# First mixer: squares' sums folded by VectorE and moved into the second row; row factors spread by one-pass products of two parts

## The reference, cut to what matters

```
def rms_norm(x, g):
    xf = x.astype(jnp.float32)
    y = xf * lax.rsqrt(jnp.mean(xf * xf, axis=-1, keepdims=True) + RMS_EPS)
    return (y * g.astype(jnp.float32)).astype(x.dtype)

hn = rms_norm(h, norm_mix[i])
qkv = (xn @ w_qkv).reshape(B, S, 3, N_HEADS, HEAD_DIM)      # A
q = apply_rope(qkv[:, :, 0], cos, sin)
...
h = rmsnorm(x, mix_norm[i])                                  # POOL
x = x + pool_mixer(h, pool_w[j], pool_b[j], pool_scale[j])
```

## Time and profile before

| | |
|---|---|
| median of 3 runs | 1062.39 us (1062.37 to 1062.58) |
| the profiled execution | 1062.58 us |
| its span, first to last instruction | 1060.8 us |
| PE busy | 1056.1 us |
| DVE busy | 835.5 us |
| ACT busy | 649.2 us |
| mean granted clock of TensorE | 1.000 |

### The profile page before, as it was taken

One profiled execution on the slowest core, in us unless ns is written; L12 is line 12 of the kernel. 1 busy time (PEld: TensorE's weight loads), 2 busy tenths in 40 slices (PEclk: granted clock), 3 DMA queues, 4 the chain that ended last, 5 costly groups with the idle time before them and its releaser, 6 DMA issues.

```text
span 1060.8 us, 16688 instructions
## 1 busy us (share of the span) xinstructions
PE 1056.1 (100%) x6764; PEld 941.3 (89%) x6764; DVE 835.5 (79%) x1329; ACT 649.2 (61%) x904; POOL 1.3 (0%) x8
## 2 busy tenths in 40 slices
PE   9999999999999999999999999999999999999998
PEld 8999888888898898888889888888988898888888
DVE  6896899786667789987667999876658768999851
ACT  7665587564367757765557577654557755766540
POOL 0000000000000000000000000000000000000000
PEclk9999999999999999999999999999999999999999
DMA  8554356555525165655652466565555533655540
GB/s 312 196 199 160 119 199 238 199 176 194 170 101 189 54 240 189 223 199 188 218 189 80 156 217 229 183 218 189 181 187 182 175 129 127 233 203 207 203 159 25
DMA packets 32237, 191.83 MB, mean 181 GB/s; under 512 B 4512, under 2 KB 6304, under 8 KB 12320
## 3 DMA queue, kind: packets, MB, share of 16 engines
q1 hardware_dynamic: 32016, 190.49, 51.2%
q10 hardware_dynamic: 144, 0.26, 0.1%
HBM read 189.69 MB, written 1.05 MB: 180 GB/s over the span
## 4 chain that ended last, share of the span: by engine, by line
PE 99%; DMA 0%; DVE 0%; ACT 0%; SPq 0%; issue 0%; DVEq 0%
PE banks L474 22%; PE TB L474 12%; PE SB L474 12%; PE banks L476 12%; PE TB L476 6%; PE SB L476 6%; PE banks L433 4%; PE banks L434 3%; PE banks L435 3%; PE banks L703 3%; PE banks L704 3%; PE banks L716 3%; PE banks L644 2%; PE banks L697 1%; PE banks L699 1%; PE banks L711 1%
## 5 line engine op out<-in xcount | busy, mean ns | idle before, releaser
L1737 DVE TENSOR_TENSOR wlo<-raw,whi 128x2048 fp32r<-128x2048 f32 (+2 forms) x180 | 395.8, 2202 | 77.3 <-ACT whi L1206 77.3
L1206 ACT ACTIVATE whi<-raw 128x2048 fp32r<-128x2048 f32 (+2 forms) x180 | 330.3, 1840 | 84.2 <-PE TB L476 24.7
L474 PE MATMUL banks<-xx,whi 128*128 128x512 f32 x752 | 262.1, 390 | 0.0
L476 PE MATMUL banks<-xx,wlo 128*128 128x256 f32 x752 | 212.2, 282 | 0.0
L474 PEld LDWEIGHTS banks<-xx,whi 128*128 128x128 f32 x752 | 141.2, 188 | 29.3
L476 PEld LDWEIGHTS banks<-xx,wlo 128*128 128x128 f32 x752 | 142.3, 189 | 0.0
L474 PE MATMUL TB<-xx,whi 128*128 128x512 f32 x336 | 117.8, 390 | 0.2 <-DVE xx L1742 0.2
L474 PE MATMUL SB<-xx,whi 128*128 128x512 f32 x320 | 111.8, 390 | 0.0
L476 PE MATMUL TB<-xx,wlo 128*128 128x256 f32 x336 | 94.8, 282 | 0.0
L474 PE MATMUL banks<-hx,whi 128*128 128x512 f32 x264 | 91.7, 390 | 0.0
L476 PE MATMUL SB<-xx,wlo 128*128 128x256 f32 x320 | 90.3, 282 | 0.0
(11 more groups left out here) (272 smaller groups left out, 2027.5 us busy)
## 6 DMA issues: line engine op xcount, KB each, us to landing
raw<-in_gate SPq DMA_DIRECT2D x44, 1024.0 KB, 4.8
raw<-in_up SPq DMA_DIRECT2D x44, 1024.0 KB, 4.8
raw<-in_down SPq DMA_DIRECT2D x32, 1024.0 KB, 4.8
raw<-in_down SPq DMA_DIRECT2D x16, 768.0 KB, 4.4
raw<-in_d_kq SPq DMA_DIRECT2D x8, 1024.0 KB, 4.9
raw<-in_a_kq SPq DMA_DIRECT2D x6, 1024.0 KB, 5.7
raw<-in_a_o SPq DMA_DIRECT2D x4, 1024.0 KB, 5.6
raw<-in_b_o SPq DMA_DIRECT2D x4, 1024.0 KB, 4.8
```

Of the source, the lines that this page charges most:

```text
L474: e.matmul(po[:, 0:512], wh[:, k, sl], a[:, kk, :, :].rearrange("p w s -> p (w s)"), start=start, stop=stop, skip_group_check=True)
L476: return e.matmul(po[:, 0:256], wl[:, k, sl], a[:, kk, 0, :], start=False, stop=stop, skip_group_check=True)
L1206: e.activation(whi[n % RING][:, 0:nk * w], raw[n % RAW][:, 0:nk * w], ACT.Copy).then_inc(s_hi, 1)
L1737: e.tensor_tensor(wlo[n % RING][:, 0:nk * w], raw[n % RAW][:, 0:nk * w], whi[n % RING][:, 0:nk * w].bitcast(F32), ALU.subtract).then_inc(s ...
```

## The change

In A, VectorE adds the two lines of `ssum` (a fold) before it splits the last quarter of weight unit 2; `norm_sums(A)` becomes the two products that B and DD use, and goes from before chunk 2 of slot 1 to the middle of chunk 1, between the products of the two token halves. In A and POOL the factor is rounded (copy into `rr`, part 0), the rest taken (part 1), both on VectorE (`norm_parts`), and `dg` becomes [128, 2, 256] fp32r: the identity scaled by each part, 256 columns each. `row` becomes two fp32r products of 256 columns that add up in `TB`. `dg` grows by 1024 bytes in a partition and `rr` takes 32 bytes behind it.

```diff
-        dg = sb("dg", [128, 2, 128])
+        dg = sb("dg", [128, 2, 256], F32R)
+        rr = sb("rr", [128, 2, 4], F32R)
...
-        FOLD = {B: 1, DD: 4}
+        FOLD = {A: 1, B: 2, DD: 5}
...
             def norm_sums(s):
                 e.wait_ge(s_ones, 1)
-                if s != A:
-                    e.wait_ge(s_fold, FOLD[s])
-                    for h in range(2):
-                        last = e.matmul(SB[:, 0, h:h + 1], ssum[:, 0, h * 128:(h + 1) * 128], ones[:, 0:1],
-                                        start=(h == 0), stop=True, skip_group_check=True)
-                    last.then_inc(s_sum, 1)
-                else:
-                    e.wait_ge(s_add, n_add(s, 3))
-                    token_sums(ssum, SB[:, 0, :]).then_inc(s_sum, 1)
+                e.wait_ge(s_fold, FOLD[s])
+                for h in range(2):
+                    last = e.matmul(SB[:, 0, h:h + 1], ssum[:, 0, h * 128:(h + 1) * 128], ones[:, 0:1],
+                                    start=(h == 0), stop=True, skip_group_check=True)
+                last.then_inc(s_sum, 1)
...
             def row(s, q):
+                e.wait_ge(s_ones_r, 1)
                 e.wait_ge(s_dg, 1 if s == A else 2)
-                e.matmul(TB[:, q, 0:128], ones[:, :], dg[:, 0, :], start=True, stop=True, skip_group_check=True)
-                e.matmul(TB[:, q, 128:256], ones[:, :], dg[:, 1, :], start=True, stop=True,
+                e.matmul(TB[:, q, 0:256], ones_r[:, :], dg[:, 0, :], start=True, stop=False, skip_group_check=True)
+                e.matmul(TB[:, q, 0:256], ones_r[:, :], dg[:, 1, :], start=False, stop=True,
                          skip_group_check=True).then_inc(s_row, 1)
...
-                        if i == 1 and k == (2 if s == A else 0):
+                        if i == 1 and k == 0 and s != A:
                             norm_sums(s)
...
                         high(i, 0, k)
+                        if i == 1 and k == 1 and s == A:
+                            norm_sums(s)
                         high(i, 1, k)
...
-            e.wait_ge(s_rc, 1)
-            for h in range(2):
-                last = e.activation(dg[:, h, :], ident, ACT.Copy, scale=rcol[:, h:h + 1])
+            e.wait_ge(s_rr, 1)
+            for part in range(2):
+                for h in range(2):
+                    last = e.activation(dg[:, part, h * 128:(h + 1) * 128], ident, ACT.Copy,
+                                        scale=rr[:, part, h:h + 1].bitcast(F32))
...
+            def norm_parts(s, col):
+
+                e.wait_ge(s_rc, COL[s])
+                kept(e.tensor_copy(rr[:, 0, 0:2], col))
+                after_own()
+                e.tensor_tensor(rr[:, 1, 0:2], col, rr[:, 0, 0:2].bitcast(F32), ALU.subtract).then_inc(s_rr, 1)
...
                     norm_col(s)
                     if s == A:
+                        norm_parts(s, rcol)
                         lo(u + 3)
...
-                norm_diag(s, ra)
+                norm_parts(s, ra[:, 0:2])
+                norm_diag(s)
...
                 if q:
                     add_squares(A, q)
+                if q == 3:
+                    e.wait_ge(s_add, n_add(A, 3))
+                    e.tensor_tensor(ssum[:, 0, :], ssum[:, 0, :], ssum[:, 1, :], ALU.add).then_inc(s_fold, 1)
                 lo_quarter(2, q)
```

More of the change, by code:

```diff
@@ L130, in build @@
         s_sq2, s_add2 = sem("s_sq2"), sem("s_add2")
+        s_rr = sem("s_rr")
         s_dg, s_row, s_rb, s_ones = sem("s_dg"), sem("s_row"), sem("s_rb"), sem("s_ones")
@@ L504, in last_pair @@
                         last.then_inc(s_half, 1)
-            def token_sums(src, dst):
-                for h in range(2):
[L508 to L511, removed]
             def norm_sums(s):
                 e.wait_ge(s_ones, 1)
-                if s != A:
-                    e.wait_ge(s_fold, FOLD[s])
-                    for h in range(2):
-                        last = e.matmul(SB[:, 0, h:h + 1], ssum[:, 0, h * 128:(h + 1) * 128], ones[:, 0:1],
-                                        start=(h == 0), stop=True, skip_group_check=True)
-                    last.then_inc(s_sum, 1)
-                else:
-                    e.wait_ge(s_add, n_add(s, 3))
-                    token_sums(ssum, SB[:, 0, :]).then_inc(s_sum, 1)
+                e.wait_ge(s_fold, FOLD[s])
[3 more added lines that the diff above has]
+                last.then_inc(s_sum, 1)
             def spread_sums(s):
@@ L1133, in both_sums @@
                     e.wait_ge(s_ones, 1)
-                    e.wait_ge(s_fold, 3)
+                    e.wait_ge(s_fold, 4)
                     for h in range(2):
@@ L1806, in norm_spread, with norm_diag @@
                 rsqrt(v, rb[:, :], rtmp[:, 1, :]).then_inc(s_rb, 1)
-            def norm_diag(s, col):
-                e.wait_ge(s_con, 16)
-                e.wait_ge(s_rc, COL[s])
-                for h in range(2):
-                    last = e.tensor_scalar(dg[:, h, :], ident, col[:, h:h + 1], None, ALU.mult)
+            def norm_parts(s, col):
[3 more added lines that the diff above has]
+                e.tensor_tensor(rr[:, 1, 0:2], col, rr[:, 0, 0:2].bitcast(F32), ALU.subtract).then_inc(s_rr, 1)
+            def norm_diag(s):
+                e.wait_ge(s_con, 16)
+                e.wait_ge(s_rr, 2)
+                for part in range(2):
+                    for h in range(2):
+                        last = e.tensor_scalar(dg[:, part, h * 128:(h + 1) * 128], ident,
+                                               rr[:, part, h:h + 1].bitcast(F32), None, ALU.mult)
                 last.then_inc(s_dg, 1)
```

## The result

The changed kernel takes 1066.95 us (median of 6 runs, 1066.56 to 1067.24), the kernel before 1062.70 beside it (6 runs, 1062.37 to 1063.68). The ratio is 1.0039, interval 1.0029 to 1.0049: slower by 4.25 us, where 0.85 us less was forecast. The profiled execution took 1066.98 us, its span is 1065.2 (before 1060.8).

A forecast was written before the change was run, and what follows sets the result against it. TensorE, busy for the whole span, was taken as the bound. Savings of 0.44 + 0.21 + 0.20 = 0.85 us, all else nothing, gave 1062.39 - 0.85 = 1061.54, given as 1061.5 us; range 1061.0 to 1065.0.

The forecast's parts named there:

- the one on the addresses: Tiles behind dg and rr move 1056 bytes; bounds from 2.2 us gain to 4.9 us cost, taken as nothing.
- Rival (b): Products with hx or ox moving (L474, L476) get slower by 2.6 to 4.9 us; 1064.1 to 1066.4; chance 0.28.
- The argument against it: The spread_sums product, moving tile 32 past a multiple of 64, is slowest per column, so the address is not the cause.
- The comparison that carried the price: Pair with hx moving, 0.3464 us, against 0.350 for 768 columns with whi moving: 3.6 ns a pair.
- The sum on TensorE: Savings at three places in A and POOL: 0.44 + 0.21 + 0.20 = 0.85 us.
- Sums of A: Near 19.7 us, eight TensorE records become four as in DD, 0.89 to 0.45 us: minus 0.44 us.
- row of A: Near 24.3 us, the row becomes two fp32r products of 256 columns, 0.45 to 0.24 us: minus 0.21 us.
- row of POOL: Near 574.8 us, 0.44 to 0.24 us: minus 0.20 us, not swallowed by TensorE's wait at F2.
- The margins: Slack before TensorE would wait: fold 0.13 us, A's factor chain 0.7, POOL's factor chain 0.4; all cost nothing.
- (a): Fold late, 0.1 to 0.3 us stall at A's sums, or POOL's 0.20 swallowed; about 1061.9; chance 0.16 with (d).
- (d): Row's products keep two passes or wait for dg; only 0.44 us saved, 1061.95; chance 0.16 with (a).
- Rival (c): The moved tiles gain TensorE time, up to 2.2 us; 1059.3 to 1061.3; chance 0.06.

The follow-up runs named there:

- weights_only: Kernel before with whi and wlo moved from 0 to 32 bytes, xx, hx and ox staying at 32 modulo 128; 1073.61 us, ratio 1.0102.
- map_3: Kernel before with hx starting 0 and ox 80 bytes past a multiple of 128; one timed execution, 1067.29 us.
- map_2: Kernel before with hx starting 16 and ox 0 bytes past a multiple of 128; one timed execution, 1064.19 us.
- after_1024: Changed kernel with rr 1024 bytes wide, so hx and ox lie 2048 bytes further than in the kernel before; 1062.04 us, ratio 0.9994.
- weights_32: Kernel before with whi and wlo moved from 0 to 32 bytes and xx, hx and ox to 96 modulo 128; 1073.12 us, ratio 1.0099.

## Why the prediction was wrong

**The step that failed** is the one on the addresses. It saw that `hx` and `ox` go from 32 past a multiple of 64 onto one, priced that at 2.6 to 4.9 us for 712 pairs, and took nothing. Measured: 6.5 ns a pair with `hx` and 5.7 with `ox`, so 616 x 6.5 + 96 x 5.7 = 4.6 us, and some 0.5 us from the products of 256 columns with the same tiles moving, which no bound had counted. Rival (b) is what happened, just above its own span of 1064.1 to 1066.4 (a price of 5.1 us, where 4.9 was the upper bound); it had a chance of 0.28, and the range was cut off within it, at 1065.0.

**The argument against it was unsound.** It read the product of rows 7, slow with its moving tile at the favoured place, as a sign that the place doesn't matter. But there the weights, `ones_r`, lie at 32 too. weights_only shows this very combination to be slow in the pairs, with 256 columns at 120.5 ns where weights at 0 have 118.3. So the row was no evidence against the effect and may well have been a second sign of it; for `spread_sums` itself no run shows which. The comparison that carried the price, `hx` against `whi` moving, came out near the truth by luck: its passes have the moving tile at 0 and the weights, `xx`, at 32, a pair of places that the change doesn't make, and with `whi` moved to 32 they stayed at 233 ns.

The kernel itself held a sign that the prediction doesn't mention: behind `con` stands a tile of 32 bytes, `pad_moving` (made by `off_line("moving")`), that nothing reads or writes. Without it `hx` and `ox` would start at 0 modulo 128, where map_3 and map_2 have 351.1 and 350.8 ns a pair.

By the Trainium skill's page "SBUF — State Buffer", section "Specifications (TRN2)", lines are 16 bytes long. From that the prediction worked out that a move by 1056 bytes is free. The runs disagree for multiples of 16 (3.3 to 6.5 ns a pair between them) and the measurement decides; that the place 36 is the slowest agrees with lines of 16 bytes.

**The sum on TensorE was right.** Sums of A minus 0.44, row of A minus 0.22, row of POOL minus 0.20, in the changed kernel itself; with the tiles 2048 bytes from their old place (after_1024) the time is lower by 0.77 us, where 0.85 was forecast, and 0.46 for the sums alone, where 0.44 was. POOL's share was not swallowed: the wait at the start of F2 is 0.18 us as before.

**The margins were right.** VectorE after (in brackets idle time and releaser), then ScalarE:

```profile
17.24 0.69 DVE L1746 TENSOR_TENSOR ssum<-ssum,sq 128x512 f32<-128x512 f32 x1
17.97 0.43 DVE L2357 TENSOR_TENSOR ssum<-ssum 128x256 f32<-128x256 f32 x1
18.31 0.69 DVE L2346 TENSOR_TENSOR wlo<-raw,whi 128x512 fp32r<-128x512 f32 x1
19.25 0.16 DVE L1777 TENSOR_SCALAR small<-SB 128x2 f32<-128x2 f32 x1 [0.25 <-PE SB L512]
...
24.25 0.42 DVE L2038 TENSOR_TENSOR hsq<-con,TB 128x256 f32<-128x256 f32 x1 [0.47 <-PE TB L528]
```

```profile
21.68 1.28 ACT L1699 ACTIVATE dg<-con,rr 128x128 fp32r<-128x128 f32 x4 [2.15 <-DVE rr L1809]
```

The fold ends at 18.40 and the sums start at 18.71 with no wait; the sums are read at 19.25 (forecast 19.29), the identity is begun at 21.68 (21.73) and ready at 22.96 (23.13), the tables begin at 24.25 (24.30, before 24.95). Rivals (a) and (d) had no part: no idle time ahead of the sums, one record for each product of the row. Rival (c) fell with (b).

**What stays open**: the rule behind the table (the moving tile's place alone doesn't give it, and its distance to the weights leaves the two levels of weights_32), why a move by 128 bytes costs the single products of 256 columns, and the late load in B.

## What to carry to other kernels

A tile that grows or is added moves every tile declared behind it, and on a kernel that is bound by TensorE for its whole span the place of a moving tile was worth six times what the change saved. Put new small tiles behind the large operands, or keep the total of added bytes such that the operands keep their places: here 128 bytes kept the pairs' pace and lost about 0.5 us elsewhere, 2048 bytes kept all. Then compare the pitch of untouched products before and after. When a row is brought as evidence against a theory, ask whether the row differs from the case in one thing only.

## What the runs showed of the hardware

With fp32r operands, a pair of 512 and 256 columns with new weights each takes 346.7 to 353.3 ns at TensorE's full granted clock (1.000), depending on where in a 128 byte stretch the moving tile and the weights start, and 357.7 ns where the start is no multiple of 16 bytes. In one execution the same places gave 348.9 and 353.3 ns in different stages. Moving by 128 or by 2048 bytes left the pairs as they were; by 128 bytes the single products of 256 columns got slower (47 steps with `ox` moving, 5.68 us in place of 5.59), by 2048 they did not. The durations of the weight loads in the groups of the page stay at 188 to 189 ns, before and after; it is the product's modelled duration (396 ns in place of 390) and the pitch from start to start that show it.
